# Paged attention: pages turned by VectorE in blocks of 32 by 32, scores in sixteen tiles of TensorE

## What is computed

```python
def mla_sample(q_nope, q_rope, new_rows, cache_l, page_table, lp):
    past = cache_l[page_table].reshape(Bd, -1, KV_CACHE_DIM)
    q_lat = jnp.einsum('bthd,chd->bthc', q_nope, lp["w_uk"])
    pc, pr = past[..., :KV_LORA_RANK], past[..., KV_LORA_RANK:]
    s_past = jnp.einsum('bthc,bkc->bhtk', q_lat, pc) + jnp.einsum('bthr,bkr->bhtk', q_rope, pr)
    ...
    s = jnp.concatenate([s_past.astype(F32), s_new], axis=-1) * MLA_SCALE
    p = jax.nn.softmax(s, axis=-1).astype(new_rows.dtype)
    ctx = jnp.einsum('bhtk,bkc->bthc', p[..., :n_past], pc) + jnp.einsum('bhtk,bkc->bthc', p[..., n_past:], nc)
    o = jnp.einsum('bthc,chd->bthd', ctx, lp["w_uv"])
```

## Time and profile before

| | |
|---|---|
| runs | 1081.27, 1081.08, 1078.83 us; median 1081.08 |
| profiled execution | 1080.94 us, span 1078.7 us, granted clock 0.981 |
| busy in the span | PE 94%, weight loads 84%, DVE 48%, ACT 28%, POOL 42% |
| stage of the change, 303 to 455 us | 14% of the span |

### The profile page before, as it was taken

One profiled execution on the slowest core, in us unless ns is written; L12 is line 12 of the kernel. 1 busy time (PEld: TensorE's weight loads), 2 busy tenths in 40 slices (PEclk: granted clock), 3 DMA queues, 4 the chain that ended last, 5 costly groups with the idle time before them and its releaser, 6 DMA issues.

```text
span 1078.7 us, 19052 instructions
## 1 busy us (share of the span) xinstructions
PE 1010.3 (94%) x8116; PEld 903.9 (84%) x8116; DVE 517.9 (48%) x723; ACT 303.7 (28%) x619; POOL 454.1 (42%) x297
## 2 busy tenths in 40 slices
PE   2899978978899999899999999999999999999997
PEld 2889967855666666599996579999999999999997
DVE  2788968358655555446225436541143124214413
ACT  3523245436444444212014412220021002001222
POOL 1554466530011111255522026555565656555561
PEclk9899989989999999999999999999999999999998
DMA  6323234540436666452239012232323233232322
GB/s 175 106 59 79 78 113 143 127 149 1 176 117 264 266 263 254 139 195 79 88 122 386 11 38 81 79 98 79 98 80 96 81 86 91 84 94 80 97 78 83
DMA packets 144009, 129.78 MB, mean 120 GB/s; under 512 B 13093, under 2 KB 136882, under 8 KB 140086
## 3 DMA queue, kind: packets, MB, share of 16 engines
q1 hardware_dynamic: 138550, 88.10, 27.1%
q0 software_dynamic: 2304, 37.75, 9.1%
q10 hardware_dynamic: 3072, 2.72, 0.8%
HBM read 123.53 MB, written 5.03 MB: 119 GB/s over the span
## 4 chain that ended last, share of the span: by engine, by line
PE 79%; DVE 9%; ACT 3%; issue 2%; DMA 2%; POOL 2%; SPq 2%; ACTq 0%; DVEq 0%; POOLq 0%
PE gps L557 55%; PE gps L861 6%; PE aux L877 3%; PE aux L897 2%; PE gps L988 1%; PE gps L1063 1%; POOL wlo L487 1%; PE aux L872 1%; PE aux L812 1%; DMA wraw<-in_w_q_up_dram 1%; PE gps L834 1%; PE aux L1001 1%; DMA wraw<-in_w_mem_v_dram 1%; PE aux L1022 1%; PE aux L887 1%
## 5 line engine op out<-in xcount | busy, mean ns | idle before, releaser
L557 PE MATMUL gps<-act_hi,whi 128*128 128x272 f32 x944 | 275.5, 292 | 8.8 <-DVE act_lo L1545 6.4
L474 POOL TENSOR_SCALAR whi<-wraw 128x1024 fp32r<-128x1024 f32 (+1 forms) x110 | 114.1, 1038 | 385.2 <-PE gps L557 276.9
L557 PE MATMUL gps<-act_lo,whi 128*128 128x272 f32 x944 | 274.5, 291 | 0.0
L557 PE MATMUL gps<-act_hi,wlo 128*128 128x272 f32 x944 | 273.9, 290 | 0.0
L477 POOL TENSOR_TENSOR wlo<-wraw,whi 128x1024 fp32r<-128x1024 f32 (+1 forms) x110 | 260.1, 2365 | 9.2
L557 PEld LDWEIGHTS gps<-act_hi,whi 128*128 128x128 f32 x944 | 179.4, 190 | 9.6 <-issue 6.4
L557 PE MATMUL gps<-h_hi,whi 128*128 128x272 f32 x640 | 185.7, 290 | 0.0
L557 PE MATMUL gps<-h_lo,whi 128*128 128x272 f32 x640 | 185.1, 289 | 0.0
L557 PE MATMUL gps<-h_hi,wlo 128*128 128x272 f32 x640 | 184.6, 288 | 0.0
L557 PEld LDWEIGHTS gps<-act_hi,wlo 128*128 128x128 f32 x944 | 179.4, 190 | 0.0
L557 PEld LDWEIGHTS gps<-act_lo,whi 128*128 128x128 f32 x944 | 179.2, 190 | 0.0
(11 more groups left out here) (356 smaller groups left out, 1496.8 us busy)
## 6 DMA issues: line engine op xcount, KB each, us to landing
wraw<-in_w_up_dram SPq DMA_DIRECT2D x32, 512.0 KB, 4.1
wraw<-in_w_down_dram SPq DMA_DIRECT2D x32, 512.0 KB, 3.9
wraw<-in_w_in_dram SPq DMA_DIRECT2D x14, 512.0 KB, 4.0
kv<-in_cache_mem_k_dram SPq DMA_DIRECT2D x7, 1024.0 KB, 7.8
kv<-in_cache_mem_v_dram SPq DMA_DIRECT2D x7, 1024.0 KB, 12.5
wraw<-in_w_mem_k_dram SPq DMA_DIRECT2D x8, 512.0 KB, 3.9
wraw<-in_w_mem_v_dram SPq DMA_DIRECT2D x8, 512.0 KB, 3.9
wraw<-in_w_out_dram SPq DMA_DIRECT2D x8, 512.0 KB, 4.3
```

What stands on the lines that cost most here:

```text
L474: nc.gpsimd.tensor_scalar(whi[:, slot, 0:n], wraw[:, slot, 0:n], 1.0, 1.0, ALU.mult, ALU.mult).then_inc(pool_step, 1)
L557: mm = nc.tensor.matmul(out_of(a), w_of(w, k), x_of(x, k, part), start=(k == 0 and s == 0), stop=(k == k_tiles - 1 and s == 2))
```

## The change

VectorE turns the pages instead of TensorE. Its transpose works on blocks of 32 by 32: in three instructions per half, each of 16 tokens times 96 columns, block (token group g of 32 partitions, token s, column block j) is turned in place, so that `cT` holds on partitions 32g to 32g+31 the 32 columns of block j for the tokens of group g. Nothing of this passes through PSUM.

The scores then contract over 32 rows at a time. Nine column blocks (eight latent, one rope) times four row groups g times four parts z of the tokens are 144 matmuls per half, each with 32 rows, 32 columns of weights and 128 moving columns. The row group is where the tokens lie, the column group is z; the output goes to partitions 32z of bank g of `gps`, so all four banks hold one half's scores. Each row group needs the queries on its own partitions: `qrA` and `qrB` hold them replicated, written by 16 new DMAs on SP from `qlat` once it is ready, while the rope part is copied by VectorE as before, into `qrB`. `qropez`, `ropc`, `ropT` and POOL's `rope_part` go.

The scores of a half are made in three thirds, `score(n, t)`, each behind the transpose `turned(n, t)`; a transpose waits for the scores of the same third of the half before, since there is one `cT`. The first third of the next half waits for the exponentials of this half (`g_exp`), since there is one set of score banks. ScalarE takes over the copy of `pTs`, now of two buffers, and of the two small tiles `pnT` and `ctxn`. POOL's next weight split waits for the last scores, since `qrA` lies in that buffer.

```diff
-        cT = at("cT", [128, 2, 2048], F32, M0 + 18432)
-        ropT = at("ropT", [128, 512], F32, M0 + 34816)
+        cT = at("cT", [128, 9, 16, 32], F32, M0 + 18432)
...
+        qrA = at("qrA", [128, 6, BD * 32], F32, W0 + 18432)
+        qrB = at("qrB", [128, 3, BD * 32], F32, M0 + 46016)
...
+            sp.wait_ge(ql_ok, 1)
+            for g in range(4):
+                r = slice(32 * g, 32 * g + 32)
+                for a in range(4):
+                    dst = qrA[r, 2 * a:2 * a + 2, :] if a < 3 else qrB[r, 0:2, :]
+                    sp.dma_start(dst, qlat[32 * a:32 * a + 32, :, :, :].rearrange("p c b q -> p c (b q)")).then_inc(qr_in, 16)
...
-                    rope_part(0)
                     pool.wait_ge(at_lo, 4)
                     gather(3)
...
+                    for i in range(NH - 4):
+                        pool.wait_ge(g_V, i + 1)
+                        gather(i + 4)
+                    pool.wait_ge(g_S, 3 * NH)
...
-            def turn(n):
...
-            def score(n):
+            def score(n, t):
 
                 b = n // 2
...
+                pe.wait_ge(g_T, 3 * n + t + 1)
+                if t == 0 and n:
+                    pe.wait_ge(g_exp, n)
+                for j in range(3 * t, 3 * t + 3):
+                    c, a = divmod(j, 4)
+                    w = qrB[:, 2, :] if j == 8 else qrA[:, 2 * a + c, :] if a < 3 else qrB[:, c, :]
+                    for g in range(4):
+                        r = slice(32 * g, 32 * g + 32)
+                        for z in range(4):
+                            mm = nc.tensor.matmul(gps[32 * z:32 * z + 32, g, 0:128],
+                                                  w[r, 32 * b:32 * b + 32],
+                                                  cT[r, j, 4 * z:4 * z + 4, :].rearrange("p s k -> p (s k)"),
+                                                  start=(j == 0), stop=(j == 8), skip_group_check=True)
                 mm.then_inc(g_S, 1)
...
-            for n in range(NH - 1):
-                turn(n + 1)
-                turn_p(n)
-                score(n + 1)
-                values(n)
+            pe.wait_ge(at_lo, 4)
+            pe.wait_ge(qr_in, 256)
+            for t in range(3):
+                score(0, t)
+            for n in range(1, NH):
+                turn_p(n - 1)
+                score(n, 0)
+                score(n, 1)
+                values(n - 1)
+                score(n, 2)
...
+                act.wait_ge(g_PT, n + 1)
+                if n >= 2:
+                    act.wait_ge(g_V, n - 1)
+                nc.scalar.copy(pTs[:, n % 2, :], aux[:, 0, :]).then_inc(g_pe, 1)
...
+            def turned(n, t):
+
+                if t == 0:
+                    dve.wait_ge(page_in[n % 4], 16 * (n // 4) + 16)
+                if n:
+                    dve.wait_ge(g_S, 3 * n + t - 2)
+                V.transpose(cT[:, 3 * t:3 * t + 3, :, :].rearrange("p j s k -> p s j k"),
+                            pg[n % 4][:, :, 96 * t:96 * t + 96].rearrange("p s (j k) -> p s j k", j=3)).then_inc(g_T, 1)
...
+            for t in range(3):
+                turned(0, t)
             for n in range(NH):
...
+                if n < NH - 1:
+                    turned(n + 1, 0)
+                dve.wait_ge(g_S, 3 * n + 3)
+                step(V.tensor_reduce(sl[:, 0, n % 2, n // 2:n // 2 + 1], gps[:, :, 0:128],
+                                     mybir.AxisListType.XY, ALU.max))
                 V.tensor_scalar(nm[:, n:n + 1], sl[:, 0, n % 2, n // 2:n // 2 + 1], -1.0, None, ALU.mult
                                 ).then_inc(g_max, 1)
                 if n < NH - 1:
...
+                    turned(n + 1, 1)
+                    turned(n + 1, 2)
```

More of the change, by code:

```diff
@@ L518, in _ @@
                     gather(2)
-                    rope_part(0)
                     pool.wait_ge(at_lo, 4)
                     gather(3)
-                    for i in range(NH):
-                        if i + 1 < NH:
-                            rope_part(i + 1)
-                        if i >= 1 and i + 3 < NH:
-                            pool.wait_ge(g_V, i)
-                            gather(i + 3)
+                    for i in range(NH - 4):
+                        pool.wait_ge(g_V, i + 1)
+                        gather(i + 4)
+                    pool.wait_ge(g_S, 3 * NH)
                 if U_MK <= u < U_QU:
@@ L906, in _ @@
             mm.then_inc(new_pe, 1)
-            score(0)
-            pe.wait_ge(new_dve, 2)
+            pe.wait_ge(new_act, 3)
             for g in range(2):
@@ L1397, in _ @@
                                              scale=1.0, accum_out=sn[:, 1, g:g + 1]).then_inc(new_act, 1)
-            def turned(n):
-                for i in range(9):
-                    k = 9 * n + i
-                    if k % 2 == 0:
-                        act.wait_ge(g_T, k + 1)
-                        dst = ropT[:, :] if i == 0 else cT[:, (i - 1) // 4, 512 * ((i - 1) % 4):512 * ((i - 1) % 4) + 512]
-                        nc.scalar.copy(dst, gps[:, (k + 1) % 4, :]).then_inc(g_ta, 1)
             def keep_ctx(n):
@@ L1409, in keep_ctx @@
                 nc.scalar.copy(ctxh[:, n, :], aux[:, 3, 0:256]).then_inc(g_cb, 1)
-            turned(0)
+            act.wait_ge(new_pe, 2)
+            nc.scalar.copy(pnT[:, :], aux[0:32, 3, 0:256]).then_inc(new_act, 1)
+            act.wait_ge(new_pe, 3)
+            nc.scalar.copy(ctxn[:, :], aux[:, 2, :]).then_inc(new_act, 1)
             act.wait_ge(row_out[0], 32)
```

88 lines of the change are left out of this document (14 added, 74 removed).

## The result

| | before | changed |
|---|---|---|
| median of 4 runs each, us | 1081.17 | 1149.51 |
| lowest and highest, us | 1078.83, 1082.67 | 1147.59, 1150.48 |
| span of the profiled execution, us | 1078.7 | 1145.6 |
| mean granted clock over the span | 0.981 | 0.939 |
| instructions of TensorE, loads and matmuls each | 8116 | 11860 |

The changed kernel is slower: ratio 1.0637, 95% interval 1.062 to 1.0654. The forecast was 1054, with a range up to 1130; both the direction and the range were missed.

The account below looks back on a forecast made before the run. TensorE, busy without a break in the paged attention, was taken as the bound. Fifteen periods of 7.06 instead of 8.86 us save 27.0, the start 0.2: 1080.9 - 27.0 - 0.2 = 1053.7, so 1054 us, range 1043 to 1130.

Parts of the forecast that it names:

- What bounds the kernel before: Paged attention: TensorE works without a break, 8.96 us per half, so time taken from it shortens the span.
- VectorE's transposes: VectorE, three per half: 1.80 us each, as a copy from PSUM, with ends 1.44 and 4.2.
- D: Rival: VectorE becomes the bound, transposes 4.2 us each, period 13.7 us, 1162 us in all; chance 0.06.
- The wait behind a last third: From a maximum's start, through the exponentials, to the hand-over to TensorE: 1.74 us per half.
- I take 9 ns: TensorE's scores: 288 pairs of load and matmul per half at 9 ns, 2.6 us; ends 2.0 and 8.1.
- B: Rival: row groups don't overlap, 28 ns per pair, scores 8.1 us, period 12.5, 1139 us; chance 0.12.
- Rival C: TensorE's scores: 13 to 22 ns per pair from feeding many instructions, period 8.2 to 10.8 us; chance 0.12.
- hidden, with 1 us of throughput to spare: Page gathers: issued 12.5 us before need against 9.2 to land, so they add no time.
- rival E: TensorE's clock falls to 1.2 GHz, its 4.77 us per period double, period 11.8, 1125 us; chance 0.07.
- The first half: 0.2 us gained: Start of the stage: the first maximum starts at 311.9 instead of 312.04, a gain of 0.2 us.
- Behind the last maximum the chain is as before: End of the stage, fold of the halves included: no change in time behind the last maximum.
- the forecast's 7.06: New period of a half, from maximum to maximum: 7.06 us against 8.86, saving 27.0 us over fifteen periods.

Follow-up runs that it names:

- e7: The kernel before, its latent score and value matmuls cut into pieces of 64 columns, about 291 pairs per half: 1129.11 us.
- e12: The changed kernel with values moved behind the last third of the scores and scores of three row groups only: 1114.36 us.
- e8: The changed kernel with the values of the half before moved behind the last third of the scores, into TensorE's wait: 1155.32 us.
- e4: The changed kernel without the gathers of halves 4 to 15, which use earlier pages again: 1121.12 us.
- e1: The changed kernel with the score matmuls of one row group only, 36 instead of 144 per half: 1107.36 us.
- e5: The changed kernel with one row group's scores only and two matmuls on constants in the wait for the exponentials: 1052.76 us.
- e6: The changed kernel without gathers after the first four halves and with two matmuls on constants in the wait: 1115.67 us.
- e3: The changed kernel with two matmuls on constants in TensorE's wait for the exponentials: 1161.72 us.
- e10: The changed kernel with four diagonal 512-column score tiles, weights turned on VectorE, values over 32 rows, all computed: 1171.95 us, ratio to before 1.0837.

## Why the prediction was wrong

- **What bounds the kernel before: right.** TensorE without a break. e7 confirms it from the other side: what delays TensorE there lengthens the period.
- **VectorE's transposes: right.** 1.80 forecast, 1.755 measured, 48 of them; it never was the bound. D fell.
- **The wait behind a last third: right.** 1.74 us from the maximum's start to that of the weights' transposes, 1.74 measured; it shows as [2.05 <-ACT ps] on TensorE:

```profile
384.52 0.42 PEld L862 LDWEIGHTS aux<-ident,ps 128*128 128x128 f32 x4 [2.05 <-ACT ps L1390]
385.11 1.20 PEld L851 LDWEIGHTS gps<-cT,qrA 32*32 32x32 f32 x95 [0.17 <-issue]
```

- **"I take 9 ns": the step that failed.** While instructions are at hand the rate is nearly that: 95 loads start within 1.20 us, less the 0.1 of the last one 12 ns apart, so 288 pairs would be 3.4 us and B's reason, row groups that do not overlap, fell (its 1139 lies nearest to the measured 1149.5, by luck). The Trainium skill, TensorE: Matmul & The Clock Gate, section Wait — 56ns, not 53.3ns?, says that starts never come closer than about 25 ns; the 12 ns measured here for tiles side by side decide against it. But 9 ns was read from 16 pairs and laid over 288 per half, with no term for bringing the instructions. The scores were to take 2.6 us per half; they keep TensorE busy for 5.6 us, at a clock of 0.75, and it stands still for 1.9 us more. What a pair more costs once TensorE has used up the blocks at hand is 35 ns beside the gathers (e12 and e8); even with nothing in their way the blocks were at least 3.2 us apart, 3.2/128 = 25 ns per pair, 8.1 us for the 324 pairs of a half, which is above the whole period that I forecast. Rival C named the mechanism ("far more instructions must be fed than in bursts of 16") and gave it 13 to 22 ns, which no row bore out: the page of before has 64 instruction packets for TensorE, from which 128 pairs to a packet could have been worked out, and what it did not show was how far apart they must be. Even the block pace that I could have read, a distance in the busiest stretch, was nowhere under 9.3 us in the stage before; the honest upper end was open, and I closed it at 28 ns.
- **The gathers "hidden, with 1 us of throughput to spare": wrong in what they delay.** They did come in time for their readers (VectorE's transposes waited 5.7 us in all, and for scores). But the instruction blocks use the same DMA engines and were not in my sum; behind a gather they are late, which costs 2.2 us a period (e4) and makes the 3 to 4.4 us stalls.
- **The clock, rival E: real, not what binds.** The clock fell, 0.75 in the stage, not to the 0.5 that E asked for. Where it decides alone, with one row group, it is worth 10.31 − 6.97 = 3.3 us a period (e1 and e5), near the 4.7 that E gave it. With all pairs, raising it gave nothing (e6 against e4, 0.06 us; e3 against the changed kernel, less than nothing). Part of the low clock seems to come from the stalls, since it reads 0.50 behind the one shown and 0.52 behind e6's; how much of the 12.93 us it costs in that way was not separated. Behind the waits of e1 the clock reads 0.50 and 0.54. These rows agree with the Trainium skill, TensorE: Matmul & The Clock Gate, section HAM oscillation — how this bites in real kernels, that waits between bursts bring the clock down each time.
- **The first half: 0.2 us gained was forecast, 4.0 lost**, by the same stall, 3.07 us, before any wait for exponentials. **"Behind the last maximum the chain is as before": wrong.** 1.9 us came on: POOL's split, which the change moved, falls on the fold, and two of VectorE's instructions there take 2.95 us instead of 0.44.
- Sum of it, from the changed kernel's 12.93 against the forecast's 7.06: e5, with few instructions and no pause, has 6.97 (6.6 in the steady state); e6, with all instructions but nothing in their blocks' way, 10.67; with the gathers it is 12.9 to 13.7 (changed kernel, e8, e3), filled or not.

## What to carry to other kernels

Count instructions per microsecond before cutting a matmul into tiles. Sixteen tiles side by side are nearly as fast as hoped in a burst (12 ns a pair), but each needs its own load and matmul (two of each in f32), and here 128 such pairs never came less than 3.2 us apart, and in the stages that ran dry every 3.8 to 4.4 us (median); a loop that wants them faster runs at the pace of its instructions, and slower still where large gathers run at the same time. Look for it in the profile as idle time of TensorE that ends on "issue", and in the count of instruction packets of the stretch; an experiment that narrows the columns at the same count, or cuts the old kernel's matmuls into pieces, shows it in one run. The plainest sign is that stalls begin at the same place of every 256 instructions.

A pause of 2 us in each half cost more through the clock than by itself (3.3 us, e1 against e5), and work put in the pause takes that cost away (e5), but only where nothing else binds: test such a remedy together with the others and not alone.

## What the runs showed of the hardware

- TensorE's instructions arrive in packets of 16 KB, 128 pairs of load and matmul. In the stage of none of the runs did two packets start less than 3.2 us apart, even with no gathers (3.20 in e4, 3.26 in e6). Whether the pace lies in the engine's asking or in the transfer (a packet took 0.9 to 1.6 us in the changed kernel) stays open. When TensorE has run dry it goes on 1.2 to 1.7 us behind a packet's landing.
- Behind a gather that keeps the DMA engines at 0.96 such a packet came 7.7 us after the one before (382.14 to 389.85); without the later gathers (e4) the period is 2.2 us shorter.
- Tiles in different row groups and different column groups run side by side without loss (e10: four matmuls of 512 columns every 0.43 us), and a quarter of the array kept the clock at 1.00.
- VectorE turns 128 by 1536 f32 in blocks of 32 by 32 in 1.755 us and 128 by 512 in 0.67 (e10).
- Two VectorE TENSOR_TENSOR instructions of 32 by 72 on SBUF, 0.22 us each by themselves, took 0.85 and 2.10 us while POOL's split ran. What passes between the two engines no run here shows.
